# A fused transformer kernel: the first channel pair of the last MLP is computed as seven quarter products, like the other ten

## The reference, cut to what matters

```python
h2 = rms_norm(x, g_mlp) * (1 + sc2) + sh2
u  = causal_dwconv(h2 @ w_up, conv_w, conv_b)      # w_up 1024 x 5632, 3 taps over the tokens
a, g = split(u, 2)                                 # 2816 channels each
x  = x + ga2 * ((silu(g) * a) @ w_down)            # w_down 2816 x 1024
out = rms_norm(x, g_final)
```

## Time and profile before

| | us |
|---|---|
| median of three runs | 1506.28 |
| profiled execution, device time | 1505.69 |
| its span in the profile | 1504.0 |
| PE busy in the span | 1304.8 |
| up projection, pairs 1 to 10 on PE | 125.07 |
| down projection on PE, in the chain | 56.67 |
| granted TensorE clock, mean | 0.948 |

### The profile page before, as it was taken

One profiled execution on the slowest core, in us unless ns is written; L12 is line 12 of the kernel. 1 busy time (PEld: TensorE's weight loads), 2 busy tenths in 40 slices (PEclk: granted clock), 3 DMA queues, 4 the chain that ended last, 5 costly groups with the idle time before them and its releaser, 6 DMA issues.

```text
span 1504.0 us, 25662 instructions
## 1 busy us (share of the span) xinstructions
PE 1304.8 (87%) x9738; PEld 807.2 (54%) x9738; DVE 664.4 (44%) x1621; ACT 274.0 (18%) x756; POOL 131.4 (9%) x201
## 2 busy tenths in 40 slices
PE   9999999766776679999999766776678999999997
PEld 4455565433443444665665433443344874899943
DVE  3874534221222123672634221222122635699976
ACT  2153211100010001372211100010001134222200
POOL 1312000000000000210100000000000143222100
PEclk9999999898898899999999998898889999999999
DMA  8978799999999999959899999999999991654400
GB/s 287 404 286 340 290 421 404 421 421 422 422 422 422 422 422 396 364 195 420 320 420 404 421 421 422 422 422 422 422 422 400 381 364 44 210 169 169 168 29 28
DMA packets 120555, 513.63 MB, mean 342 GB/s; under 512 B 12296, under 2 KB 46796, under 8 KB 69144
## 3 DMA queue, kind: packets, MB, share of 16 engines
q1 hardware_dynamic: 118576, 507.30, 84.4%
q0 software_dynamic: 1728, 5.12, 0.9%
q10 hardware_dynamic: 168, 0.09, 0.0%
HBM read 511.39 MB, written 1.08 MB: 341 GB/s over the span
## 4 chain that ended last, share of the span: by engine, by line
PE 53%; DMA 20%; SPq 18%; DVE 3%; issue 3%; POOL 1%; ACT 1%; ACTq 0%; POOLq 0%; DVEq 0%
DMA ring<-in_moe_w_up 14%; SPq L1872 13%; PE bank L1415 9%; PE bank L2678 8%; PE bank L575 7%; PE bank L2713 4%; DMA BC<-in_moe_w_up 3%; PE bank L1430 3%; PE bank L1401 3%; PE bank L453 3%; PE bank L2303 3%; PE bank L465 3%; SPq L1881 3%; PE bank L1443 2%; DMA ring<-in_moe_w_down 2%
## 5 line engine op out<-in xcount | busy, mean ns | idle before, releaser
L1415 PE MATMUL bank<-ring,hT 128*32 128x256 f32 (+1 forms) x2848 | 280.5, 461 | 133.4 <-DMA ring<-in_moe_w_up 70.3
L1415 PEld LDWEIGHTS bank<-ring,hT 128*32 128x32 f32 (+1 forms) x2848 | 148.5, 133 | 238.9 <-issue 180.7
L1707 DVE TENSOR_SCALAR pT<-pT 128x256 f32<-128x256 f32 x34 | 10.0, 294 | 407.4 <-ACT pT L1839 407.4
L1415 PE MATMUL bank<-BC,hT 128*32 128x256 f32 (+1 forms) x1120 | 138.6, 410 | 41.8 <-DMA ring<-in_moe_w_up 24.3
L1401 PEld LDWEIGHTS bank<-gtab,hn 128*128 128x128 f32 x1088 | 129.3, 192 | 15.4 <-issue 14.3
L1401 PE MATMUL bank<-gtab,hn 128*128 128x128 f32 x1088 | 132.6, 275 | 0.1
L1430 PE MATMUL bank<-ring,gtab 128*32 128x512 f32 (+1 forms) x768 | 116.8, 596 | 1.9 <-DMA ring<-in_moe_w_down 1.4
L1443 PE MATMUL bank<-hT,A 128*128 128x512 f32 x256 | 118.3, 605 | 0.0
L1415 PEld LDWEIGHTS bank<-BC,hT 128*32 128x32 f32 (+1 forms) x1120 | 72.1, 120 | 76.2 <-issue 57.4
L575 PE MATMUL bank<-ring,hT 128*128 128x512 f32 (+3 forms) x288 | 99.9, 505 | 0.7 <-DMA ring<-in_diff_w_in 0.4
L1839 ACT ACTIVATE pT<-bank 128x256 f32<-128x256 f32 x34 | 13.1, 384 | 460.5 <-PE bank L1415 460.5
(11 more groups left out here) (390 smaller groups left out, 1942.3 us busy)
## 6 DMA issues: line engine op xcount, KB each, us to landing
ring<-in_moe_w_gate SPq DMA_DIRECT2D x90, 1024.0 KB, 25.1
ring<-in_moe_w_up SPq DMA_DIRECT2D x88, 1024.0 KB, 25.5
ring<-in_moe_w_down SPq DMA_DIRECT2D x88, 1024.0 KB, 26.2
BC<-in_moe_w_gate SPq DMA_DIRECT2D x38, 1024.0 KB, 24.8
BC<-in_moe_w_up SPq DMA_DIRECT2D x32, 1024.0 KB, 25.0
BC<-in_moe_w_down SPq DMA_DIRECT2D x28, 1024.0 KB, 26.6
ring<-in_w_ada SPq DMA_DIRECT2D x24, 1024.0 KB, 13.9
ring<-in_w_up SPq DMA_DIRECT2D x22, 1024.0 KB, 7.6
```

The costliest lines, as they stand in the source:

```text
L1415: i = nc.tensor.matmul(GATE[q * cap:(q + 1) * cap, part * FF:(part + 1) * FF], xg[:, c, q * cap:(q + 1) * cap], u[:, c, :], start=(c == 0) ...
```

## The change

Pair 0 becomes seven quarter products like the rest. PE multiplies the raw products (0 and 1) of pairs 0 and 1 ahead of the turn of tile 1, and after the turn pair 0's products 4, 3, 5, 2, 6, then pair 1's 2 to 6, then whole pairs. DVE forms pair 0's first weight sums ahead of the scaling of tile 1 (`sums_ahead` step 0), and its second sums, the copy of the turned taps (L2824 before) and its fourth sums between the scaling and the evacuation of tile 1 (step 1). It joins pair 0 behind the sums of pair 1. ACT keeps product 0 of pair 0 between squaring and evacuating tile 1. POOL forms differences for pair 0, too, and starts with them without waiting for the turned taps; the two pairs that it has done at once are now 0 and 1, and not 1 and 2. Token sums are signalled one by one. Banks rotate by one pair further, so P1 to P7 move to other banks; P1's is again that of the last pair's product 4. Semaphore counts follow. Not shown: the renumbered counts (`formed_s1` and so on), the five functions that return a product's operands, and `second_sums` and `fourth_sums`, whose bodies are the old lines.

```diff
-        def close_vector(dve, products, norm, first_added=True):
+        def close_vector(dve, products, norm, first_added=True, ahead=None):
...
             products.add(dve, 1, 1)
+            if ahead:
+                ahead(dve, 0)
             norm.scale(dve, 1)
+            if ahead:
+                ahead(dve, 1)
             norm.evac(dve, 1, 0)
 
-        def close_scalar(act, norm):
+        def close_scalar(act, norm, amid=None):
             for tt in range(TT):
                 norm.square(act, tt)
+                if amid and tt == 1:
+                    amid(act)
                 norm.evac(act, tt, 1)
...
-        P1, P2, P3, P4, P5, P6, P7 = (bank[b] for b in (5, 6, 0, 1, 2, 3, 4))
+        P1, P2, P3, P4, P5, P6, P7 = (bank[b] for b in (4, 5, 7, 0, 1, 2, 3))
...
-            return bank[(2 + 7 * (j - 1) + k) % 8]
+            return bank[(2 + 7 * j + k) % 8]
...
+        first_order = ((0, 0), (0, 1), (1, 0), (1, 1), (0, 4), (0, 3), (0, 5), (0, 2), (1, 2), (1, 3), (1, 4), (1, 5))
...
         def thirds_gpsimd(pool):
-            pool.wait_ge(*cw_turned3(1))
-            for j in range(1, PAIRS):
-                if j >= 3:
+            for j in range(PAIRS):
+                if j == 1:
+                    pool.wait_ge(*cw_turned3(1))
+                if j >= 2:
                     pool.wait_ge(*done_with(up_units[j - 2][1]))
...
-            def up(n, b, t0, t1):
-                w = units[up_units[0][n]][0](slot(up_units[0][n]))
-                for c in range(DC):
-                    if n == 0 and b == 0 and t0:
-                        n4.column(pe, 1, c)
-                    i = nc.tensor.matmul(bank[n][:, b * S + t0:b * S + t1], w[:, c, b * P:(b + 1) * P],
-                                         hT[:, c, t0:t1], start=(c == 0), stop=(c == DC - 1))
-                return i
-            for n in range(2):
-                if n == 1:
-                    o3.ready(pe, 1)
-                unit_here(pe, up_units[0][n])
-                for b in range(2):
-                    if n == 1 and b == 1:
-                        n4.turn(pe, 1)
-                    up(n, b, 0, P)
-            for n in range(2):
-                for b in range(2):
-                    i = up(n, b, P, S)
-                i.then_inc(unit_done.sem, 1)
-            pe.wait_ge(*cw_out(1))
...
-            for j in range(1, PAIRS):
+            def raw_products(j):
                 for h in range(2):
                     unit_here(pe, up_units[j][h])
-                if j >= 3:
+                if j >= 2:
                     pe.wait_ge(*up_added(added_c21(j - 2)))
                 product_of(j, 0, [up_part_of(j, h, 0, 0) for h in range(2)], tokens_of(0, 0))
-                if j >= 2:
+                if j >= 1:
                     pe.wait_ge(*up_copied(copied_p1(j - 1)))
                 product_of(j, 1, [up_part_of(j, h, 0, 1) for h in range(2)], tokens_of(1, 0))
...
+            raw_products(0)
+            o3.ready(pe, 1)
+            raw_products(1)
+            n4.turn(pe, 1)
+            pe.wait_ge(*up_formed(formed_s4(0)))
+            n4.tile(pe, 1)
+            product_of(0, 4, *fourth_weights(0))
+            pe.wait_ge(*up_formed(formed_tokens(0)))
+            product_of(0, 3, *first_weights(0))
+            pe.wait_ge(*up_third(1))
+            pe.wait_ge(*up_formed(formed_tokens(2)))
+            product_of(0, 5, *third_weights(0))
+            pe.wait_ge(*cw_out(1))
+            pe.wait_ge(*up_formed(formed_tokens(1)))
+            product_of(0, 2, *second_weights(0))
+            pe.wait_ge(*up_formed(formed_tokens(3)))
+            product_of(0, 6, *last_weights(0))
+            for j in range(1, PAIRS):
+                if j >= 2:
+                    raw_products(j)
                 pe.wait_ge(*up_formed(formed_s2(j)))
...
+                pe.wait_ge(*up_added(added_c11(j - 1)))
+                product_of(j, 2, *second_weights(j))
+                pe.wait_ge(*up_added(added_c12(j - 1)))
+                product_of(j, 3, *first_weights(j))
                 pe.wait_ge(*up_formed(formed_s4(j)))
-                if j >= 2:
-                    pe.wait_ge(*up_added(added_c22(j - 1)))
-                product_of(j, 4, [up_sum(j, 2, h) for h in range(2)], tokens_of(1, 1))
...
-                product_of(j, 6, [up_part_of(j, h, 1, 1) for h in range(2)], token_sums[3])
+                pe.wait_ge(*up_added(added_c22(j - 1)))
+                product_of(j, 4, *fourth_weights(j))
+                pe.wait_ge(*up_third(j + 1))
+                product_of(j, 5, *third_weights(j))
+                product_of(j, 6, *last_weights(j))
             pe.wait_ge(*up_added(added_c12(PAIRS - 1)))
...
+        def keep_first(act, j):
+            act.wait_ge(*up_part(part(j, 0)))
+            nc.scalar.activation(first_kept[j % 2], two_rows(part_bank(j, 0)[:, 0:S]), ACT.Copy).then_inc(up_copied.sem, 1)
...
-            for h in range(2):
-                act.wait_ge(*done_with(up_units[0][h]))
-                nc.scalar.activation(raw[:, 0, h, :], bank[h][:, :], ACT.Copy).then_inc(up_copied.sem, 1)
+            keep_first(act, 1)
             act.wait_ge(*cw_out(1))
             for j in range(1, PAIRS + 1):
                 if j >= 2:
                     act.wait_ge(*hid3(j - 1))
-                    act.wait_ge(*up_added(added_c21(j - 1)))
-                else:
-                    act.wait_ge(*up_copied(2))
+                act.wait_ge(*up_added(added_c21(j - 1)))
                 taps(j - 1)
-                if j < PAIRS:
-                    act.wait_ge(*up_part(part(j, 0)))
-                    nc.scalar.activation(first_kept[j % 2], two_rows(part_bank(j, 0)[:, 0:S]), ACT.Copy).then_inc(up_copied.sem, 1)
+                if 2 <= j < PAIRS:
+                    keep_first(act, j)
...
+        def first_sums(dve, j):
+            for h in range(2):
+                unit_here(dve, up_units[j][h])
+            if j >= 2:
+                dve.wait_ge(*done_with(up_units[j - 2][1]))
+            for h in range(2):
...
+        def sums_ahead(dve, step):
+            if step == 0:
+                first_sums(dve, 0)
+                return
+            second_sums(dve, 0)
+            dve.wait_ge(*cw_turned3(1))
+            nc.vector.tensor_copy(cw3, bank[4][:, 0:256].rearrange("p (k b) -> p k b", k=4)[:, :, 0:2 * FB_]
+                                  ).then_inc(cw_out.sem, 1)
+            fourth_sums(dve, 0)
...
                 n4.tile(dve, tt)
-            nc.vector.tensor_tensor(token_sums[0], tokens_of(0, 1), tokens_of(0, 0), ALU.subtract)
-            dv.done(nc.vector.tensor_tensor(token_sums[2], tokens_of(1, 1), tokens_of(0, 1), ALU.subtract))
-            dv.done(nc.vector.tensor_tensor(token_sums[1], tokens_of(1, 1), token_sums[0], ALU.subtract))
+            nc.vector.tensor_tensor(token_sums[0], tokens_of(0, 1), tokens_of(0, 0), ALU.subtract).then_inc(up_formed.sem, 1)
+            nc.vector.tensor_tensor(token_sums[2], tokens_of(1, 1), tokens_of(0, 1), ALU.subtract).then_inc(up_formed.sem, 1)
+            dve.wait_ge(*up_formed(formed_tokens(0)))
+            nc.vector.tensor_tensor(token_sums[1], tokens_of(1, 1), token_sums[0], ALU.subtract).then_inc(up_formed.sem, 1)
+            dve.wait_ge(*up_formed(formed_tokens(1)))
             nc.vector.tensor_tensor(token_sums[3], token_sums[1], tokens_of(1, 0), ALU.subtract).then_inc(up_formed.sem, 1)
-            first_sums(1)
-            fourth_sums(1)
+            first_sums(dve, 1)
+            second_sums(dve, 1)
+            join_11(0)
+            fourth_sums(dve, 1)
+            join_u2(0)
+            join_u4(0)
+            join_12(0)
+            join_2(0)
...
                 if j < PAIRS - 1:
-                    first_sums(j + 1)
+                    first_sums(dve, j + 1)
+                    second_sums(dve, j + 1)
```

More of the change, by code:

```diff
@@ L2604, in up_sum, with formed_tokens @@
             return up_sums[j % 2][2 * k + h]
+        first_order = ((0, 0), (0, 1), (1, 0), (1, 1), (0, 4), (0, 3), (0, 5), (0, 2), (1, 2), (1, 3), (1, 4), (1, 5))
         def part(j, k):
-            return 6 * (j - 1) + k + 1
+            return first_order.index((j, k)) + 1 if j < 2 else 6 * j + k + 1
         def formed_s1(j):
-            return 3 * j - 1
+            return 3 * j + (5 if j else 1)
         def formed_s2(j):
-            return 3 * j
+            return formed_s1(j) + 1
         def formed_s4(j):
-            return 3 * j + 1
+            return formed_s1(j) + 2
+        def formed_tokens(k):
+            return 4 + (0, 2, 1, 3)[k]
         def added_c11(j):
-            return 4 * j - 3
+            return 4 * j + 1
         def added_c12(j):
-            return 4 * j - 2
+            return 4 * j + 2
         def added_c22(j):
-            return 4 * j - 1
+            return 4 * j + 3
         def added_c21(j):
-            return 4 * j
+            return 4 * j + 4
         def copied_tap(j, h):
-            return 3 * j + 3 + h
+            return 3 * j + h + (2 if j else 3)
```

(45 more changed lines are left out.)

31 lines of the change are left out of this document (3 added, 28 removed).

## The result

The changed kernel takes 1511.35 us (median of 7 runs, 1510.42 to 1512.01); the kernel before, run beside it, 1506.09 (1505.41 to 1506.65). The ratio is 1.0034, 95% interval 1.0025 to 1.0044: 5.3 us slower. The forecast was +1.8, and its range ended at 1510.4. The profiled execution took 1510.42, its span 1508.7, so 4.7 more than before's; this execution is 0.8 us ahead when it reaches this stage (the last product of the attention's output ends that much earlier), so the stage itself is 5.5 slower.

A forecast was written before the change was run, and what follows sets the result against it. PE was taken to bound the kernel, with DVE a close second. Front +0.4 and end +1.4 made +1.8 on 1505.69, 1507.5; the median's 0.59 gave 1508.1 us, range 1505.6 to 1510.4.

The forecast's parts named there:

- the turn loses its cover: Turn of tile 1: no raw matmuls stand behind it, so PE waits 1.6 to 1.9 us or more, taking back 1.79.
- fourth sums take 3.2 beside POOL: Pair 0, before tile 1's evacuation: DVE's two fourth sums meet POOL's differences and end at 1298.1, the evacuation at 1299.5.
- POOL can hold the gate: Pair loop: POOL's first operation holds DVE's gate for 1.1 us, though no row showed the gate beside POOL.
- the lag behind PE after pair 1: Pair loop: DVE finishes pair 1's last join 5.5 us after PE's product 6, and the lag stays.
- Second sums: 1293.4 to 1294.7: DVE's list behind the scaling of tile 1: pair 0's two second sums, over before POOL's differences hold anything.
- the front: The turn of tile 1 and pair 0: PE reaches product 2 of pair 1 0.4 us later than before.
- rival 4: Pauses of 2.1 and 1.4: the clock falls to 1.2 GHz, adding 1.75 to the forecast, 1509.8 us; chance 0.04.
- the end: Ahead of the down projection: iteration 10 begins 4.8 behind PE, so P1's first matmul waits 1.4 us for join_12(10).
- T_10: The moment PE ends product 6 of pair 10; P1's eleventh matmul was put at T_10 + 8.27 plus 1.4.
- 1: Pair loop: the gate isn't held, DVE sheds the lag, only the front's +0.4 is left, 1506.7 us; chance 0.15.
- 2: Whole stage: POOL and DVE meet only where both read the weight ring, not slower, 1506.3 us; chance 0.08.
- 3: Pair loop: DVE becomes the bound at 12.95 a turn, PE follows it, 1511.7 us; chance 0.11.

The follow-up runs named there:

- experiment 9: The changed kernel with only pair 0's second sums moved ahead of the scaling of tile 1: 1506.82 against 1506.00 us before, +0.8.
- Experiment 2: The changed kernel with POOL's differences held back until DVE has evacuated tile 1, its DMA issues left in place: 1508.63 against 1506.12 us before, +2.5.
- Experiment 1: The changed kernel with four unused 128x512 multiplications put into PE's pause behind the turn of tile 1: 1509.48 against 1506.12 us before, +3.4.
- experiment 5: The changed kernel with POOL's three DMA issues moved behind its differences of pair 1, without any wait: 1510.80 against 1506.12 us before, +4.7.
- experiment 6: The changed kernel with product 1 of pair 1 (8 matmuls) moved behind the turn of tile 1: 1511.70 against 1506.12 us before, +5.6.
- experiment 3: Experiment 2 with POOL's three DMA issues also moved behind the differences of pair 1: 1508.65 us, +2.5 against the kernel before.
- 4: Experiment 3 with P1 in a bank free earlier and the wait for join_12(10) behind P1's eleven matmuls: 1507.76 us, +1.6 against the kernel before.
- 7: Experiment 6 with POOL's pair 0 differences between the roots, pair 1's after DVE's evacuation, second sums ahead of the scaling: 1505.34 against 1506.12 us before, -0.8.
- 8: 7 with P1 in the bank free earlier and the wait for join_12(10) behind P1's eleven matmuls: 1504.47 us, -1.65 against the kernel before.
- 10: Experiment 9 with product 1 of pair 1 behind the turn and P1 in the bank free earlier: 1505.75 against 1506.00 us before, -0.25.

## Why the prediction was wrong

**Right:** the matmul's price and the eight saved; that the turn loses its cover, and that ACT alone would leave nothing of the gain (experiment 9: pause 1.75 against 1.79 saved); that fourth sums take 3.2 beside POOL (3.18) and the evacuation waits for them; that POOL can hold the gate (1.37 for 0.69 in pair 1), for which no row stood; the lag behind PE after pair 1 (forecast 5.5; measured 1326.45 - 1321.07 = 5.4), and that it isn't shed; that PE isn't held inside the loop; and that the next place is P1's first matmul. SP and ACT played no part.

**The step that failed** is the line "Second sums: 1293.4 to 1294.7", priced at 1.29 as if alone. They took 3.43, 2.1 more. By the trace of before I took POOL's start at 1294.63 (1293.84 in the changed kernel's trace, which is 0.8 ahead) for the moment from which it holds DVE. Unheld, the two would have been over at about that moment. But the first was held from its start at 1292.56 on, while POOL's record shows only DMA issues, and the difference behind them first at 1293.84. Experiment 2 shows that the issues alone don't hold it; experiment 9 that this step, with the clock that fell by it, was the error at the front: with the second sums out of POOL's reach the front gives and takes nothing, and the kernel is at +0.8, a little under the forecast's +1.8.

**What followed from it** is rival 4, given 0.04. It was weighed for pauses of 2.1 and 1.4; at 3.9 the clock did fall. Experiment 1 gives its price: 1.9 by medians, 23 x 0.10 = 2.3 by the records of one execution. It isn't a fixed one: in the traces of experiments 5 and 6, behind nearly the same pause, 68 and 66 records start in the first 9 us and not 59, so it was some 0.9 and 0.7 less there. The pauses of 2.0 between matmul starts in experiments 2, 3, 4 and 9 left the clock at 1.00, those of 4.0 to 4.2 in the changed kernel, 5 and 6 didn't. The rival rested on one pause of the expert stage. The same trace of before has longer ones there, and behind this one, PE's wait of 3.5 us, the clock did fall:

```profile
389.40:393.00 3.60, 0.07 (x4) 0.02 (x1) 1.86 (x6) 0.60 (x1) 0.00 (x0) 1.00 1.01 419
393.00:398.30 5.30, 5.29 (x64) 3.28 (x64) 0.00 (x0) 0.00 (x0) 0.00 (x0) 0.68 1.01 422
```

They would have told what to expect behind a pause of 3.9; at the forecast's 2.1 they change nothing.

**A size that was off:** the end. Iteration 10 began 4.0 behind PE (1425.10 - 1421.12), not 4.8, as the lag shrank from 5.4 behind pair 1 to 4.8 behind pair 4 and stood there. The balance was not the one forecast (gate held by 1.1, fourth sums by 0.87, back to 5.5 from both sides): it settled where the gate is free and the fourth sums take both meetings, 3.33 for 1.29, which the prediction thought would bring the lag back up. PE's first down matmul was 0.65 late, not 1.4. Taking the wait out gave back 0.9 in both pairs of runs (3 to 4, 7 to 8), 0.2 more than the trace shows; that remainder is within the runs' scatter and isn't settled. A reading was off without effect: P1's eleventh matmul stands at T_10 + 8.7, ten matmuls of 0.859 behind the first (56.67 / 66), and not at 8.27.

The account of the profiled execution: pause 3.9 - 1.79 = +2.1; clock +2.3; end +0.65; sum +5.1, of the stage's 5.5; 0.4 is not placed. By medians +5.3. Against the forecast the front's pause is 1.7 over, the clock 2.3 over, the end 0.75 under.

**The rivals.** 1 and 2 fell. 1 had the gate free, and from pair 2 on it was, but the fourth sums were held in its place and the lag stayed. 2 had POOL and DVE meet only at the weight ring, but the gate of pair 1, which reads `A`, was held, and so were the token sums of experiment 3. 3 gave about the right size, 1511.7, for a wrong reason: DVE was never the bound in the loop; PE's only waits are the two shown.

**Not settled:** why a POOL operation queued directly behind DMA issues holds DVE a microsecond before its recorded start. It isn't a single case: experiments 1 and 6 show the same, and in 9 and 10 it is the first fourth sum that is held (in 9 it took 1.51 from 1294.59 on; alone it would have been over at 1295.3, and the difference is recorded from 1295.61). With a wait between the issues and the difference (2, 7, 8) it doesn't happen. POOL's recorded starts are rough, so the start may be recorded late; no run separates the two.

## What to carry to other kernels

Work moved beside a wait is free only if nothing that can hold it works there. Here that was POOL, for DVE's sums with both operands in SBUF: lay POOL's list over DVE's for the whole gap, from the first instruction queued and not from the first recorded start, and price each such sum at the held duration. Ask of every pause that an edit makes what the clock does behind it if the pause comes out twice as long, and look at more than one pause of the trace for the answer; here the clock's 2.3 us was the largest part of the miss. Cover on PE is worth something only when what it covers is on time (experiment 6 against 8).

## What the runs showed of the hardware

- A DVE operation of 128x512 with both inputs in SBUF takes 1.75 us for 0.69 when it alternates with POOL's 128x512 operations, and POOL's take 1.70 each for 1.27 (four took 6.62). The scaling of a 128x1024 tile with one SBUF tile as input was held, too: 1.68 for 0.75 (experiment 5). The evacuation from PSUM wasn't (1.36, 1.35).
- POOL's DMA issues alone hold no such sum: 1.29 for two beside three issues (experiment 2). The Trainium skill, "SBUF — State Buffer", section "Who interferes with whom", infers that such a sum doesn't disturb the generation of DMA descriptors on POOL, as it takes only the read half of the port pair that the two engines share. The run agrees from both sides: the issues took 1.03, 0.53 and 0.53, as in the kernel before.
- POOL's tiny operations are held as well: the root's two (128x1) took 0.71 and 0.88 beside DVE's second sums, 0.20 and 0.56 alone, so the scaling started 0.8 later in experiments 7 to 10 (1293.67 in 9 against 1292.80 in 2, with the same start of the stage within 0.05).
- After 3.9 us of waiting TensorE ran at 1.2 GHz for 5 us of matmuls in the changed kernel's trace, and for less in those of experiments 5 and 6 (mean granted clock in the 9 us behind the pause 0.72, against 0.84 and 0.81); after 1.8 it stayed at 2.4 GHz (experiments 2, 3 and 9).
